# 256-token operand tiles of a two-block transformer at SBUF distances of their own from the weights: merged 256 bytes, FFN 64, second block's normalized 320, weighted 448, branches 128

## The reference

```
# block 1, each layer
h  = modulate(rms_norm(x), ...)                    # 1024 wide
qa, ka, va, qb, kb, vb, ga, gb = split(h @ w_in)
x += gt1 * ((sigmoid(ga)*(ya@w_pa) + sigmoid(gb)*(yb@w_pb)) @ w_out)
x += gt2 * ((silu(h2@w_gate) * (h2@w_up)) @ w_down)   # 2816 wide
# block 2, each layer
h  = rms_norm(x) * norm_w
p  = h @ w_in                                      # 18 parts, 3072 of them merge gates
y_a = sparse latent attention; y_b = stick-breaking attention; y_c = mLSTM
proj = branches @ w_branch                         # 3 branches, 512 wide
x += (sum(sigmoid(merge) * proj)) @ w_out
```

## Time and profile before

| | |
|---|---|
| median of 3 runs | 2029.8 us |
| profiled execution | 2026.5 us |
| its span, first to last instruction | 2025.0 us |
| mean granted TensorE clock | 0.985 |
| PE busy | 1936.0 us, 96% |
| DVE, ACT, POOL busy | 53%, 43%, 16% |

### The profile page before, as it was taken

The page is one execution under the profiler, slowest core; times in us unless marked ns, Lnnn a source line. Parts: engine busy times, 40 slices in busy tenths (PEclk is TensorE's granted clock), DMA queues, the critical chain, the costliest instruction groups (busy, mean ns, idle before and its releaser), DMA issues. The chain is left out here.

```text
span 2025.0 us, 30816 instructions
## 1 busy us (share of the span) xinstructions
PE 1936.0 (96%) x12540; PEld 1612.1 (80%) x12540; DVE 1075.4 (53%) x2048; ACT 874.2 (43%) x1518; POOL 333.3 (16%) x158
## 2 busy tenths in 40 slices
PE   6999999999999999989989999999999999999996
PEld 3765576877888888676889999988788899788896
DVE  4335655524111111337866556779546776864676
ACT  3213444524222322324555445446464554655453
POOL 0221222343444443310000000100001001000100
PEclk9999999999999999999999999999999999999999
DMA  8333411235223222633236555543333455233341
GB/s 346 132 120 107 157 60 63 73 125 193 99 93 103 95 94 94 222 123 134 84 115 234 182 192 183 173 161 105 132 110 123 140 175 176 100 130 105 125 136 63
DMA packets 76700, 272.28 MB, mean 134 GB/s; under 512 B 8208, under 2 KB 11536, under 8 KB 76560
## 3 DMA queue, kind: packets, MB, share of 16 engines
q1 hardware_dynamic: 74656, 266.37, 38.3%
q10 hardware_dynamic: 1904, 3.94, 0.5%
HBM read 269.23 MB, written 1.05 MB: 133 GB/s over the span
## 5 line engine op out<-in xcount | busy, mean ns | idle before, releaser
L956 PE MATMUL bank<-h,high 128*128 128x256 f32 (+1 forms) x2272 | 744.8, 328 | 15.9 <-DVE h L2246 4.1
L957 PE MATMUL bank<-h,high 128*128 128x256 f32 (+1 forms) x2272 | 708.7, 312 | 0.0
L958 PE MATMUL bank<-h,low 128*128 128x256 f32 (+1 forms) x2272 | 708.4, 312 | 0.0
L1352 ACT ACTIVATE high<-raw 128x1024 fp32r<-128x1024 f32 x408 | 426.0, 1052 | 209.2 <-PE bank L958 206.9
L956 PEld LDWEIGHTS bank<-h,high 128*128 128x128 f32 x2272 | 430.3, 189 | 105.0 <-issue 62.2
L1749 DVE TENSOR_TENSOR low<-raw,high 128x1024 fp32r<-128x1024 f32 x287 | 356.4, 1246 | 203.5 <-ACT high L1352 201.9
L957 PEld LDWEIGHTS bank<-h,high 128*128 128x128 f32 x2272 | 432.1, 190 | 25.6 <-issue 1.7
L958 PEld LDWEIGHTS bank<-h,low 128*128 128x128 f32 x2272 | 430.6, 190 | 26.5
L1683 POOL TENSOR_TENSOR low<-raw,high 128x1024 fp32r<-128x1024 f32 x121 | 293.8, 2434 | 559.5 <-ACT high L1352 559.5
L1692 POOL TENSOR_TENSOR few<-few,halves 128x2 f32<-128x2 f32 (+2 forms) x27 | 27.0, 998 | 744.0 <-DVE few L1851 744.0
L1793 DVE TENSOR_TENSOR gt<-bank,gt 128x512 f32<-128x512 f32 (+1 forms) x44 | 24.5, 558 | 194.1 <-PE bank L958 194.1
(11 more groups left out here) (291 smaller groups left out, 2777.3 us busy)
## 6 DMA issues: line engine op xcount, KB each, us to landing
raw<-stream SPq DMA_DIRECT2D x504, 512.0 KB, 3.3
xc<-x_in SPq DMA_DIRECT2D x1, 1024.0 KB, 5.4
xc<-ctx_in SPq DMA_DIRECT2D x1, 1024.0 KB, 7.6
out<-xc ACTq DMA_DIRECT2D x1, 1024.0 KB, 4.5
cst<-consts ACTq DMA_DIRECT2D x1, 896.0 KB, 6.0
cst<-consts ACTq DMA_DIRECT2D x1, 704.0 KB, 4.2
ukw<-uk ACTq DMA_DIRECT2D x1, 512.0 KB, 5.0
uvw<-uv ACTq DMA_DIRECT2D x1, 512.0 KB, 5.9
```

Of the source, the lines that this page charges most:

```text
L956: mm(dst, wh, xh, start=start, stop=False)
L957: mm(dst, wh, xl, start=False, stop=False)
L958: return mm(dst, wl, xh, start=False, stop=stop)
L1352: do(high[:, i % PAIRS, :], raw[:, slot % SLOTS, :], ACTF.Copy).then_inc(S["hi"], 1)
```

## The change: allocations only

Four kinds of unused tensors are added, each inside the scope of the tile that it shifts, so that mostly that tile alone moves; `apart_h` stands in block 2's own scope, so all that is allocated after it in block 2 moves by its 128 bytes.

```
             attn.close()
+            if l:
+                sb("apart_M", [P, 16], scope=merge)
             M[l] = [sb(f"M{i}_{l}", [P, KT, n], F32R, scope=merge) for i in range(2)]
             merge.close()
             scope.close()
+            if l:
+                sb("apart_hid", [P, 96], scope=ffn)
             hid[l] = [sb(f"hid{i}_{l}", [P, FC, n], F32R, scope=ffn) for i in range(2)]
...
         ubuf = sq2
+        sb("apart_h", [P, 32], scope=block2)
         hh2, hl2 = (sb(f"h2_{i}", [P, KT, SEQ], F32R, scope=block2) for i in range(2))
...
             early = ExitStack()
+            sb(f"apart_U{l}", [P, 32], scope=early)
             U[l] = [sb(f"U{i}_{l}", [P, KT, SEQ], F32R, scope=early) for i in range(2)]
...
             attn.close()
+            sb(f"apart_B{l}", [P, 80], scope=merge)
             B[l] = [sb(f"B{i}_{l}", [P, 12, SEQ], F32R, scope=merge) for i in range(2)]
```

## The result

The changed kernel took 2033.2 us (median of 20 runs, 2027.0 to 2036.6) against 2028.4 for the kernel before (20 runs, 2021.4 to 2033.8). The ratio is 1.0019, with an interval of 1.0010 to 1.0028: slower by 3.9 us, where 5.0 faster was forecast. The loss lies just under the 0.2% at which the chances were parted, yet its interval excludes no change. The granted clock tells the two apart by less than executions differ among themselves: its mean over the 20 runs of the changed kernel is 0.983, and over the kernel before it is 0.982 to 0.984 in each of the four series of runs recorded with the experiments.

The account below looks back on a forecast made before the run. TensorE's matmuls plus small gaps were taken as the bound. Of 11.8 us possible gain, half was taken, less 15 in 100 lost to waits: 5.0 us off 2029.8 gives 2024.8 us, with 1 in 10 left below 2017.5 and above 2036.

Parts of the forecast that it names:

- What bounds, and the paces: TensorE's matmuls set the time; 256-token matmuls have steady paces of 113.3 and 117.6 ns, and 120.4 at distance 0.
- hid to 64: hid's 528 matmuls, all at 281 ns, moved from 192 to 64: gain at most 2.3 us, loss none.
- carried on to gate and up: 528 unmoved gate and up matmuls between hid's sweeps may follow hid to 276 ns: 2.3 us gained, or nothing.
- `h` to 320: Block 2's 3072 `h` matmuls, 192 to 320: gain at most 5.3 us, loss at most 7.9; the deciding term.
- rival two: Block 2's `h` at 320 settles at the slow pace: slower, 2038.4 us at full price less hid's gain; chance 0.25.
- Reading 279 as a mixture of 276 and 281: Durations between 276 and 281 ns taken as slow shares, 0.6 in one stretch of block 2's `h`, 0.2 in another.
- M to 256: M's 192 matmuls, at 276 ns, moved from 192 to 256: no gain, loss at most 0.8 us.
- B to 128: B's 576 matmuls, 0.6 of them at 281 ns, moved from 192: gain at most 1.5 us, loss at most 1.0.
- U to 448: U's 480 matmuls, 0.2 of them at 281 ns, moved from 192: gain at most 0.4 us, loss at most 1.7.
- SV and MV: 3 x 64 matmuls with `h` as loaded operand, distance 320 to 192: nothing; 1.5 us at the best duration seen.
- The attention of block 2: Some 500 matmuls whose operands move by 128 bytes: worth 2.2 us to either side, taken as 0.
- Rival one: Distance doesn't choose the pace, new addresses only reshuffle it: 0.1 us gained, 2029.7 us; chance 0.34.

Follow-up runs that it names:

- h_alone: Changed kernel with only block 2's `h` and its scope moved, to 320; M, hid, U, B at 192: 2031.2 us against 2025.6 before, ratio 1.0016.
- mb_alone: Kernel before with only M at 256 and B at 128; `h`, hid, U at 192: 2026.3 us against 2025.6, ratio 0.9999.
- kick_once: Kernel before plus one two-column matmul ahead of the fourth gate and up tile, block 1's second layer: 2029.9 us, ratio 1.0016.

## Why the prediction was wrong

- **What bounds, and the paces: right.** The time follows TensorE's spacing, and 113.3, 117.8 and 120.0 ns, as the finer starts have it, come back in the kernels that followed; distances of 128 and unlike pairs add paces between them.
- **hid to 64, "can only win by the two paces": wrong in size.** It gained 0.0 of 2.3 us. At 64 a product takes 353 ns from every quiet start. Nothing was carried on to gate and up, so that term of 2.3 us is 0 too.
- **`h` to 320: wrong in sign, and the step that failed.** I took half of what could go, because the slow pace is "no rule of the shape". It isn't, but its share follows the distance modulo 256, and 320 is 64: fast products fell from 54% to 17%. Why 64 has fewer of them isn't known. The term was to be about 2.3 us of gain and is 4.6 us of loss. The row that said so was there: V at distance 320, 353 ns for every product, against U at 192 with 340. I gave it to rival two.
- **Reading 279 as a mixture of 276 and 281: wrong away from 192.** At 64 and 320 it is the label of the slow pace itself; only starts tell.
- **M to 256: a risk named, and met by a pace I had kept for the extreme.** 283 and 120 ns, 1.1 us. Distance 0 was in the earlier trace rows; that 256 equals 0 I didn't ask.
- **B to 128: pace lost 1.4 us, not the time.** The wait for `mg` fell from 7.7 to 6.2 us. I had discounted gains for such waits, but not losses.
- **U to 448: right at no change**, as 448 is 192 modulo 256.
- **SV and MV: taken at nothing, 0.3 us. The attention of block 2: right at nothing.** DVE, ACT and POOL are busy for the same time, and all matmuls of block 2 outside `product`, each counted to the next start and at most 600 ns, take 150.5 us before, 150.3 after and 149.6 in h_alone (my working). So its addresses cost nothing that shows.
- **Rival one (a mere reshuffle)** would allow 4.8 us between medians by luck, but not h_alone and mb_alone, in which the share follows the tile's own distance. **Rival two** was the mechanism: right place, right sign. Its price was too high, 9.6 us with U, against 4.6 for `h` alone, because a sixth of the products stayed fast and U stayed too.
- **The sum of the terms, and its luck.** 4.6 + 1.4 + 1.1 + 0.2 + 0.3 - 1.5 (the wait) is 6.1 us, less 1.1 for unmoved tiles 5.0; the medians differ by 4.8 and the ratio says 3.9. That they agree so well is partly luck, for the terms are taken from two executions whose spans differ by 0.5 us: PE is busy for 4.1 us more and idle for 3.6 less. Of the 3.6 the wait for `mg` is 1.5; waits for `tmp` (5.7 to 5.1), `h` (4.1 to 3.8) and `hsq` (7.3 to 7.0) shrank as well. How much of that belongs to the change, and how much to these two executions, stays open.

## What to carry to other kernels

Where weight loads run beneath moving operands of 256 columns, the address of the moving operand modulo 256 bytes against the weights' is worth up to 6% of a matmul (120.0 against 113.3 ns): in this kernel's shape avoid 0 and 128, and prefer 192 to 64. Read the pace from starts, not from durations, and test one distance for all tiles in a kernel that does nothing else before giving each tile its own. Where TensorE already waits for another engine, as B does for `mg`, a tile gains or loses next to nothing by it (mb_alone, 2026.3 against 2025.6 us).

## What the runs showed of the hardware that was not expected

- At distance 192 one and the same stream of matmuls has two steady paces, 340 and 353 ns for a product, kept until a short matmul or a stall, the slower one for 180 us. Which of the two follows could be neither told nor chosen. DVE at 79% and ACT at 84% busy made no difference.
- Best and worst depend on length: 512-token operands run best at distance 0 (389 ns, and 228.0 ns of spacing for SV and MV with `h` at 256 against 233.3 with it at 320), 256-token ones worst.
- The granted clock differs from one execution to the next, 0.978 to 0.988 for runs of the kernel before that took 2015 to 2034 us. Over 76 of them the time falls by 1.2 us for each 0.001 of clock (my fit, correlation -0.70; about half of the scatter is left). In kick_once, at 0.980, there are five stretches in block 2, near 1565, 1633, 1739, 1934 and 2002 us, that the kernel before didn't have in its profile. Two of them in kick_once (window, its length, PE busy and matmuls, granted clock, DMA share, GB/s):

```profile
1630.00:1637.00 7.00, 6.25 (x40) 0.76 0.50 157
1931.00:1938.00 7.00, 5.89 (x37) 0.76 0.40 148
```

and the same windows in the kernel before:

```profile
1630.00:1637.00 7.00, 7.00 (x62) 1.00 0.51 174
1931.00:1938.00 7.00, 7.00 (x58) 1.00 0.25 80
```

A mean of 0.76 says that about half of these 7 us ran at the lower level, 1.2 GHz, where successive starts are 213 ns apart. Ahead of the first of the two TensorE had waited 2.1 us for `h` (until 1630.8), which also takes 0.75 us out of its row; the kernel before has the same wait of 2.1 us (until 1629.4) with no fall behind it. By the fit, the range of the clock goes with 12 us, more than this change is worth.
